# Weight slots 64 bytes further apart, and one product of ones for each feed-forward norm

## The reference, cut to what matters

```python
def rmsnorm(x, g):
    xf = x.astype(jnp.float32)
    xf = xf * lax.rsqrt(jnp.mean(xf * xf, axis=-1, keepdims=True) + EPS)
    return xf.astype(x.dtype) * g
...
        x = x + merged @ w_out[l]
        h = rmsnorm(x, norm_ffn[l])
        g, u = jnp.split(h @ w_ffn_in[l], 2, axis=-1)
        x = x + (jax.nn.silu(g) * u) @ w_ffn_out[l]
```

## Time and profile before

| | |
|---|---|
| median of 2 runs | 2251.51 us (2250.73 to 2252.28) |
| time of the profiled execution | 2250.29 us |
| its span, first to last instruction | 2248.5 us |
| granted TensorE clock over the span | 1.000 |
| TensorE matmul busy | 2226.2 us (99%) |
| GpSimd, VectorE, ScalarE busy | 1485.3, 1030.5, 618.8 us |

### The profile page before, as it was taken

How to read it: one execution, slowest core, us unless ns; L and a number is a source line. 1 busy time by engine, 2 the same in 40 slices (tenths; PEclk the granted TensorE clock), 3 DMA queues, 4 the chain that set the end, 5 groups by cost and what they waited for, 6 DMA issues and landing times.

```text
span 2248.5 us, 33383 instructions
## 1 busy us (share of the span) xinstructions
PE 2226.2 (99%) x12339; PEld 1794.7 (80%) x12339; DVE 1030.5 (46%) x1570; ACT 618.8 (28%) x1103; POOL 1485.3 (66%) x1452
## 2 busy tenths in 40 slices
PE   8999999999999999999999999999999999999999
PEld 7777888888888897778788888888977668888887
DVE  6975745532330049759555333310494565333200
ACT  4335334221110033353442211110334553111100
POOL 6654876866766756548768667667593337776673
PEclk9999999999999999999999999999999999999999
DMA  5321334232333333213343333323330103233322
GB/s 190 103 75 57 114 122 150 94 103 94 95 101 94 96 118 103 75 58 113 123 141 104 103 94 94 102 93 95 120 117 14 38 1 112 94 94 101 94 95 84
DMA packets 69870, 217.53 MB, mean 97 GB/s; under 512 B 8448, under 2 KB 10752, under 8 KB 69632
## 3 DMA queue, kind: packets, MB, share of 16 engines
q1 hardware_dynamic: 54016, 188.41, 26.7%
q10 hardware_dynamic: 15744, 27.52, 3.4%
HBM read 195.93 MB, written 10.49 MB: 92 GB/s over the span
## 4 chain that ended last, share of the span: by engine, by line
PE 95%; DVE 2%; ACT 2%; issue 1%; ACTq 0%; DMA 0%; POOL 0%; DVEq 0%; POOLq 0%
PE ps L1769 84%; PE ps L2314 1%; PE ps L2042 1%; PE ps L2056 1%; PE ps L2147 1%; PE ps L2071 1%; PE ps L2370 1%; ACT pe L1094 1%; PE ps L1992 1%; PE ps L2337 1%; DVE small L1419 0%; PE ps L2245 0%; PE ps L2015 0%; PE ps L2176 0%; PE ps L2192 0%
## 5 line engine op out<-in xcount | busy, mean ns | idle before, releaser
L561 POOL TENSOR_TENSOR w_lo<-w_raw,w_hi 128x512 fp32r<-128x512 f32 x700 | 959.2, 1370 | 58.4
L558 POOL TENSOR_SCALAR w_hi<-w_raw 128x512 fp32r<-128x512 f32 x700 | 505.2, 722 | 593.0 <-DMA w_raw<-wst 550.7
L1769 PE MATMUL ps<-h_hi,w_lo 128*128 128x512 f32 (+1 forms) x2056 | 804.6, 391 | 3.0 <-DVE h_lo L1228 2.6
L1769 PE MATMUL ps<-h_hi,w_hi 128*128 128x512 f32 (+1 forms) x2056 | 783.8, 381 | 0.0
L1769 PE MATMUL ps<-h_lo,w_hi 128*128 128x512 f32 (+1 forms) x2056 | 783.6, 381 | 0.0
L1769 PEld LDWEIGHTS ps<-h_hi,w_lo 128*128 128x128 f32 x2056 | 386.5, 188 | 100.9 <-issue 19.8
L1769 PEld LDWEIGHTS ps<-h_lo,w_hi 128*128 128x128 f32 x2056 | 386.7, 188 | 78.4 <-issue 7.4
L1769 PEld LDWEIGHTS ps<-h_hi,w_hi 128*128 128x128 f32 x2056 | 386.5, 188 | 74.9
L1769 PE MATMUL ps<-a_hi,w_lo 128*128 128x512 f32 (+1 forms) x572 | 213.7, 374 | 0.0
L1769 PE MATMUL ps<-a_hi,w_hi 128*128 128x512 f32 (+1 forms) x572 | 213.2, 373 | 0.0
L1769 PE MATMUL ps<-a_lo,w_hi 128*128 128x512 f32 (+1 forms) x572 | 213.2, 373 | 0.0
(11 more groups left out here) (309 smaller groups left out, 2508.8 us busy)
## 6 DMA issues: line engine op xcount, KB each, us to landing
w_raw<-wst SPq DMA_DIRECT2D x350, 512.0 KB, 3.6
rot<-raw ACTq DMA_DIRECT2D x70, 128.0 KB, 3.3
gates<-gt ACTq DMA_DIRECT2D x32, 256.0 KB, 4.1
stage<-gates ACTq DMA_DIRECT2D x32, 256.0 KB, 4.2
x_sb<-xin SPq DMA_DIRECT2D x8, 256.0 KB, 5.4
out<-x_sb SPq DMA_DIRECT2D x8, 256.0 KB, 4.5
kc<-cst ACTq DMA_DIRECT2D x1, 1056.0 KB, 5.2
kc<-cst SPq DMA_DIRECT2D x1, 417.0 KB, 8.0
```

What stands on the lines that cost most here:

```text
L558: eng.tensor_scalar(w_hi[s][:, part], w_raw[s][:, part], 1.0, 1.0, ALU.mult, ALU.mult)\
L561: eng.tensor_tensor(w_lo[s][:, part], w_raw[s][:, part], w_hi[s][:, part].bitcast(F32), ALU.subtract)\
L1769: m = eng.matmul(o, w, x, start=first and i == 0, stop=final and i == 2)
```

## The change

The distance of the six weight slots goes from 8 KB to 8 KB and 64 bytes; inside a slot nothing moves. Everything that stands behind them (the tables, the constants, `rstd`, the work area with `a_hi`, `a_lo`, `ssum` and `sqb`) is 512 bytes higher. For each of the three feed-forward norms (the odd n), VectorE adds the square of tile 7 to `ssum` too, at the end of its work on the norm, and TensorE makes one product of ones instead of two; this product now stands behind block 1 of `g1` instead of before block 6 of `g0` and `u0`. The norms before the mixers keep their two products for each half of the tokens.

```diff
 def sums_before(n):
-    return (KT - 2) * (n - 1)
+    return (KT - 2) * (n - 1) + n // 2
...
-        w_raw = [sbt(f"w_raw{i}", 48 + 8 * i, 1024) for i in range(WSLOTS)]
-        w_lo = [sbt(f"w_lo{i}", 48 + 8 * i, 1024, dt=F32R) for i in range(WSLOTS)]
-        w_hi = [sbt(f"w_hi{i}", 52 + 8 * i, 1024, dt=F32R) for i in range(WSLOTS)]
-        cos_t, sin_t = sbt("cos_t", 96, T), sbt("sin_t", 98, T)
-        rstd = sbt("rstd", 100, T)
+        w_raw = [sbt(f"w_raw{i}", 48 + 8.0625 * i, 1024) for i in range(WSLOTS)]
+        w_lo = [sbt(f"w_lo{i}", 48 + 8.0625 * i, 1024, dt=F32R) for i in range(WSLOTS)]
+        w_hi = [sbt(f"w_hi{i}", 52 + 8.0625 * i, 1024, dt=F32R) for i in range(WSLOTS)]
+        cos_t, sin_t = sbt("cos_t", 96.5, T), sbt("sin_t", 98.5, T)
+        rstd = sbt("rstd", 100.5, T)
...
-        WK = 107.25
+        WK = 107.75
...
                     for j in range(4 if l == L2 else KT - 1, KT):
                         scaled_rest(n + 1, j)
+                    add_square(n + 1, KT - 1)
...
-            def gemm(name, x_h=h_hi, x_l=h_lo):
+            def gemm(name, x_h=h_hi, x_l=h_lo, then={}):
...
                     m = product(o, *weights(c, k), x_h[:, k, :], x_l[:, k, :], k == 0, k == KT - 1)
+                    if k in then:
+                        then[k]()
...
                 o = bank(6) if half is None else bank(6 + half, 0, HALF)
+                if n % 2:
+                    eng.wait_ge(sum_done, sums_before(n) + KT - 1)
+                    eng.matmul(o, ones, ssum[:, :], start=True, stop=True).then_inc(ms_done, 1)
+                    return
                 eng.wait_ge(sum_done, sums_before(n) + KT - 2)
...
                 for k in range(KT):
-                    if k == KT - 2:
-                        mean_square(2 * l + 1)
                     eng.wait_ge(h_ready, tiles_before(2 * l + 1) + k + 1)
...
-                for n in ("g1", "u1"):
-                    gemm((l, n))
+                gemm((l, "g1"), then={1: lambda: mean_square(2 * l + 1)})
+                gemm((l, "u1"))
```

More of the change, by code:

```diff
@@ L254, in program @@
         h_lo = sbt("h_lo", 32, KT, T, dt=F32R)
-        w_raw = [sbt(f"w_raw{i}", 48 + 8 * i, 1024) for i in range(WSLOTS)]
-        w_lo = [sbt(f"w_lo{i}", 48 + 8 * i, 1024, dt=F32R) for i in range(WSLOTS)]
-        w_hi = [sbt(f"w_hi{i}", 52 + 8 * i, 1024, dt=F32R) for i in range(WSLOTS)]
-        cos_t, sin_t = sbt("cos_t", 96, T), sbt("sin_t", 98, T)
-        rstd = sbt("rstd", 100, T)
-        kc = sbt("kc", 102, C_W)
-        vecs = sbt("vecs", 106.28125, V_W)
-        small = sbt("small", 106.625, 128)
-        WK = 107.25
+        w_raw = [sbt(f"w_raw{i}", 48 + 8.0625 * i, 1024) for i in range(WSLOTS)]
[3 more added lines that the diff above has]
+        rstd = sbt("rstd", 100.5, T)
+        kc = sbt("kc", 102.5, C_W)
+        vecs = sbt("vecs", 106.78125, V_W)
+        small = sbt("small", 107.125, 128)
+        WK = 107.75
         f_sb = sbt("f_sb", WK, 4, T)
@@ L323, in program @@
         vmz = sbt("vmz", WK + 40.5, P)
-        kept = [sbt(f"kept{i}", 96 + 2 * i, T) for i in range(KEPT)]
+        kept = [sbt(f"kept{i}", 96.5 + 2 * i, T) for i in range(KEPT)]
         osq2, ors2 = sbt("osq2", WK, T), sbt("ors2", WK + 2, T)
```

## The result

The changed kernel takes 2273.22 us (2273.08 to 2273.36, 2 runs) against 2251.51 us. The ratio is 1.01 with a 95% interval of 1.0084 to 1.0116: 1% slower, 22 us, where 2.6 us less was forecast. Its span is 2271.2 us, 22.7 us more than before.

What follows compares the result with a forecast made beforehand. The prediction took TensorE's matmul count times their distance to bound the kernel. Three norms saving 0.86 us each gave -2.6 us, all else 0, so 2251.51 - 2.6 = 2248.9 us, range 2245 to 2253 us.

Steps and rivals of the forecast that it cites:

- What bounds the kernel: Whole kernel: time is the number of TensorE matmuls times the distance from one to the next, 0.2267 us for 512 columns.
- One product of ones fewer: Three feed-forward norms: one of two products on TensorE's path goes, saving 0.86 us each, -2.6 us.
- The slots, TensorE's distance: Moved weight slots: distance between matmuls taken not to depend on place, 0 us; bounds were 13.4 ns given back or doubled.
- the remainder: Each float32r matmul: the 13.4 ns of its distance beyond the 0.2133 us that 512 columns take at 2.4 GHz.
- the range: Whole kernel: 2245 us (forecast less run spread and a tenth of a nanosecond per matmul) to 2253 us (no gain, small loss).
- a longer distance: TensorE's matmuls: slower case, sharing a chance of 0.04 with late weights, of which 0.03 beyond 2%.
- late weights: Rival: GpSimd splits slower in moved slots; at 1.6 times, 119 us more, 2370 us; chance 0.04 shared with longer distance.
- signs of being wrong: Distance off 0.2267 us or differing between slots; GpSimd's idle time vanishing; a gap before block 7 of `g0`/`u0` or `g2`.
- The rival of a shorter distance: 64 bytes spare TensorE 13.4 ns for 5/6 of 8004 matmuls: 89 us gain, 2162 us; chance 0.04, small part 0.03.
- The moved product: Product of ones behind block 1 of `g1`: `rstd` 3.2 us later, 4.0 us margin before `g2`; cost 0, at most 1 us.
- The last `h_lo` without its cover: Third layer's norm, block 7: last `h_lo` arrives with 0.87 us to spare; cost 0, some 0.2 us if unlucky.
- the added additions: VectorE, end of three norms: one addition each, covered by 1.8 us at worst; cost 0, at most 1.8 us uncovered.

Runs made afterwards that it cites:

- norm alone: The changed kernel with the slots 8 KB apart again (what follows stays 512 bytes higher), only the norm part left: 2248.24 us, ratio 0.9988 to the kernel before.

## Why the prediction was wrong

**What bounds the kernel** was right: TensorE's matmuls times their distance. All of the loss went through that distance.

**One product of ones fewer** was right: 0.86 us each, -2.6 us forecast, -2.7 us measured by the norm alone. That the totals agree to 0.1 us is partly luck. The interval allows a gain of 0.7 to 4.7 us, the kernel lost 0.4 us before `g2` (below), and its waits for `h_lo` (L1228), in stages that the change doesn't touch, were 2.0 instead of 2.6 us.

**The slots, TensorE's distance** is the step that failed: "I take 0, by the rows that agree to a tenth of a nanosecond". The rows were right, but for `a_hi` standing 1.25 KB and not a quarter of a KB beyond a multiple of 2 KB, and the conclusion went beyond them. Every relative place in the old kernel was a multiple of 256 bytes, h tiles, a tiles and all blocks of weights alike; they agreed because they were all the same case. The prediction had written that nothing shows steps of 64 bytes, and had set the bounds at the remainder given back or doubled, then kept only the end of no effect for the range. In its place the runs show 6.6, 5.8, 2.9, 0.4 and 6.6 ns more for each matmul in the slots at 64, 128, 192, 256 and 320 bytes, and 1.2 ns in slot 0, which follows the last of them; 25 us in all. The upper bound, 13.4 ns for each matmul, held; the range did not reach to it. The chance of a longer distance shared 0.04 with late weights and was not a rival of its own. One of the prediction's signs of being wrong, a distance that differs between slots, came true, and so did a gap before `g2`.

**The rival of a shorter distance** asked the right question and got the sign wrong. None of the places tried is better than the old one. Its argument for itself, an obstacle met once for each load of weights, isn't borne out either: 64 bytes add 6.6 ns with 512 columns and take 2.2 ns away with 256, and loading fewer columns doesn't lower the distance below 226.7 ns. The Trainium skill (TensorE: Matmul & The Clock Gate, Step-by-step: what each phase is for) says that loading the next tile's weights doesn't steal SBUF read bandwidth from the running matmul. The runs don't agree with two reads that leave each other alone: with the same instructions and nothing else running, the place of the two operands alone moves the distance from 226.7 to 233.3 ns. Which of the two reads is held up, no run shows.

**Late weights** did not occur. Over the whole kernel the splits took 713 and 1372 ns in the mean against 722 and 1370 before, and the loads 3.6 us as before; GpSimd is not among TensorE's waits.

**The moved product** was mis-sized: taken as 0, it cost 0.4 us. The margin of 4.0 us before `g2` of the first layer was in fact gone. The timeline of TensorE, norm alone:

```profile
462.57 0.39 PE L1770 MATMUL ps<-h_hi,w_hi 128*128 128x512 f32 x1
463.21 0.50 PE L1770 MATMUL ps<-h_hi,w_lo 128*128 128x512 f32 x1 [0.25 <-DVE fs L1336]
```

The step is 0.64 us instead of 0.23, so 0.4 us was lost. The cause is in VectorE's timeline, changed kernel:

```profile
460.26 0.63 DVE L1263 TENSOR_TENSOR small<-small 128x4 f32<-128x4 f32 x1 [8.96 <-ACT small L630]
...
461.70 1.16 DVE L1267 TENSOR_TENSOR small<-small 128x4 f32<-128x4 f32 x1
...
467.01 0.69 DVE L1336 TENSOR_TENSOR fs<-ps,rstd 128x512 f32<-128x512 f32 x1 [0.23 <-DVE small L1273]
```

and in GpSimd's at the same time:

```profile
461.54 1.30 POOL L561 TENSOR_TENSOR w_lo<-w_raw,w_hi 128x512 fp32r<-128x512 f32 x1
```

The same steps in the kernel before, in VectorE's timeline:

```profile
453.05 0.16 DVE L1263 TENSOR_TENSOR small<-small 128x4 f32<-128x4 f32 x1 [7.41 <-ACT small L630]
...
453.85 0.16 DVE L1267 TENSOR_TENSOR small<-small 128x4 f32<-128x4 f32 x1
```

From the first of the small steps to `rstd`'s first use it is 6.75 us; before, it was 2.4 us (455.49 less 453.05), when GpSimd happened to be idle (until 456.94, by its timeline). Moved by some microseconds they met its splits: L1267, 0.16 us before, now lasts 1.16 us and ends at 462.86, just behind the split that began before it and ends at 462.84. Six more of the ten steps became longer (L1263, L1265, L1268, L1270, L1271, L1273), and each of them, too, ends within 0.03 us of the end of a split. I had shifted the old times instead of asking what they would meet. The upper bound of 1 us covered it.

**The last `h_lo` without its cover** and **the added additions** cost nothing, as written: no entry of either among TensorE's waits.

**The range** should have held the upper bound of the unknown distance. On 8004 matmuls, 13.4 ns are 107 us, and even a quarter of that is outside. Its lower end, 2245 us, is also about 1 us lower than its two terms give, 2248.9 - 1.6 - 1.2 = 2246.1 us; nothing hung on that.

## What to carry to other kernels

Where TensorE is busy throughout, the distance between the starts of matmuls is the first thing to read before and after a change of layout; here the sum by slot showed where the time went. For float32r products of 512 columns with 128 columns of weights loaded each time, keep weights and moving tiles at the same place within 256 bytes; for other shapes the best place was another, so measure before padding. Rows that all agree say nothing about cases that none of them contains: ask what they have in common before taking them for independence.

## What the runs showed of the hardware

- The distance between float32r matmuls of 512 columns with 128 x 128 weights depends on the start of the weights relative to the moving tile, within 256 bytes: 226.7 ns at 0, 233 to 234 ns at 32 to 96, 232 to 233 ns at 128, 233 ns at 160 and 224, 229 ns at 192. This holds where all matmuls of a sequence stand alike. With weights and h tiles both 64 bytes up it was 226.7 ns again, so neither operand's own address showed an effect.
- With 256 columns the same places give 120.0 ns at 0 and 117.8 ns at 64, with TensorE alone.
- Where a slot in step follows one out of step, three to six matmuls pass until the distance is steady. One kind of weights at 64 bytes costs a triple 13.2 ns, twice one pair's surplus, and one mixed arrangement costs nothing. So the distance is a property of the sequence, not a sum over matmuls. The mechanism is open: an experiment with fewer columns to load contradicted both a collision that lasts as long as the load and a fixed price.
- VectorE's steps on 128 x 4 elements took up to 1.16 us instead of 0.16 while GpSimd split weights, each long one ending within 0.03 us of the end of a split.
- No place that was tried gives less than 226.7 ns, 13.4 ns over 512 columns at 2.4 GHz.
